# Gated-unit products: weights stationary, or tokens stationary with three products and transposes

## The reference, cut to what matters

```
def swiglu(x, w_gu, w_down):
    g, u = jnp.split(x @ w_gu, 2, axis=-1)      # w_gu: 1024 x 5632
    return (jax.nn.silu(g) * u) @ w_down        # w_down: 2816 x 1024

x = layer_norm(ALPHA * x + 0.5 * swiglu(x, ...), ...)   # four times
```

## Time and profile before

| | us |
|---|---|
| median of 3 runs | 1352.56 (1352.48 to 1353.29) |
| the profiled execution's own time | 1351.47 |
| its span, first to last instruction | 1349.7 |
| PE busy | 1325.7 (98%) |
| PEld busy | 1114.7 (83%) |
| DVE busy | 879.0 (65%) |
| ACT busy | 699.9 (52%) |
| mean granted TensorE clock | 0.997 |

### The profile page before, as it was taken

The page is one execution under the profiler, slowest core; times in us unless marked ns, Lnnn a source line. Parts: engine busy times, 40 slices in busy tenths (PEclk is TensorE's granted clock), DMA queues, the critical chain, the costliest instruction groups (busy, mean ns, idle before and its releaser), DMA issues.

```text
span 1349.7 us, 17387 instructions
## 1 busy us (share of the span) xinstructions
PE 1325.7 (98%) x6757; PEld 1114.7 (83%) x6757; DVE 879.0 (65%) x1214; ACT 699.9 (52%) x1116; POOL 76.1 (6%) x114
## 2 busy tenths in 40 slices
PE   6999999999999999999999999999999999999997
PEld 6788878888888888888877888888888888888885
DVE  6787668777667665665447664676654676766464
ACT  3675564453444554555665553555554544455452
POOL 1401101000002000001001000001000010100000
PEclk9999999999999999999999999999999999999999
DMA  9957754557556655646516556556655565665641
GB/s 349 317 198 242 278 182 162 187 212 257 187 202 192 198 187 185 197 173 225 187 63 218 188 187 211 193 169 219 205 177 183 187 224 182 212 194 187 199 170 69
DMA packets 160222, 268.45 MB, mean 199 GB/s; under 512 B 9755, under 2 KB 103052, under 8 KB 160012
## 3 DMA queue, kind: packets, MB, share of 16 engines
q1 hardware_dynamic: 152428, 239.47, 52.4%
q0 software_dynamic: 7648, 27.85, 5.9%
q10 hardware_dynamic: 64, 0.02, 0.0%
HBM read 266.21 MB, written 1.07 MB: 198 GB/s over the span
## 4 chain that ended last, share of the span: by engine, by line
PE 94%; DVE 2%; DMA 1%; ACT 1%; POOL 1%; issue 0%; SPq 0%; DVEq 0%; ACTq 0%; POOLq 0%
PE TBB L842 12%; PE UPP L842 12%; PE Y L790 10%; PE Y L791 10%; PE Y L792 10%; PE UPP L790 7%; PE UPP L792 7%; PE UPP L791 7%; PE UPP L843 6%; PE TBB L843 6%; PE TBB L887 2%; PE Y L919 1%; DMA WADA<-in_w_ada 1%; PE Y L926 1%; DVE ADA L1847 0%; DMA ADA<-in_b_ada 0%
## 5 line engine op out<-in xcount | busy, mean ns | idle before, releaser
L1726 DVE TENSOR_TENSOR WL<-RAW,WH 128x1024 fp32r<-128x1024 f32 (+2 forms) x438 | 502.3, 1193 | 169.9 <-ACT WH L1307 166.0
L1307 ACT CAST WH<-RAW 128x1024 fp32r<-128x1024 f32 (+2 forms) x438 | 424.6, 1025 | 204.7 <-PE Y L792 73.5
L842 PE MATMUL UPP<-AHL,WH 128*128 128x512 f32 x672 | 240.5, 400 | 0.0
L842 PE MATMUL TBB<-AHL,WH 128*128 128x512 f32 x672 | 239.1, 398 | 0.0
L790 PE MATMUL Y<-WH,HH 128*128 128x512 f32 (+1 forms) x496 | 192.1, 387 | 0.0
L792 PE MATMUL Y<-WH,HL 128*128 128x512 f32 (+1 forms) x496 | 191.4, 386 | 0.0
L791 PE MATMUL Y<-WL,HH 128*128 128x512 f32 (+1 forms) x496 | 191.3, 386 | 0.0
L843 PE MATMUL UPP<-AHL,WL 128*128 128x256 f32 x672 | 188.6, 281 | 0.0
L843 PE MATMUL TBB<-AHL,WL 128*128 128x256 f32 x672 | 188.6, 281 | 0.0
L790 PE MATMUL UPP<-WH,AHL 128*128 128x512 f32 (+1 forms) x448 | 183.1, 409 | 2.4 <-DVE AHL L1880 1.2
L792 PE MATMUL UPP<-WH,AHL 128*128 128x512 f32 (+1 forms) x448 | 174.8, 390 | 0.0
(11 more groups left out here) (258 smaller groups left out, 1370.8 us busy)
## 6 DMA issues: line engine op xcount, KB each, us to landing
RAW<-in_ffn_w_gu SPq DMA_DIRECT2D x176, 512.0 KB, 4.9
RAW<-in_ffn_w_down SPq DMA_DIRECT2D x80, 512.0 KB, 4.3
RAW<-in_w_mlp SPq DMA_DIRECT2D x64, 512.0 KB, 4.4
RAW<-in_w_in SPq DMA_DIRECT2D x34, 512.0 KB, 5.1
PIECE<-in_w_ada POOLq DMA_DIRECT2D x32, 512.0 KB, 5.6
RAW<-in_a_w_in SPq DMA_DIRECT2D x24, 512.0 KB, 4.7
WADA<-in_w_ada SPq DMA_DIRECT2D x14, 512.0 KB, 10.1
RAW<-in_w_out SPq DMA_DIRECT2D x8, 512.0 KB, 4.5
```

The source lines that it names most:

```text
L842: pe.matmul(banks[:, block, :], WH[:, u % 2, w], AHL[:, k, :], start=k == 0, stop=False)
L1307: act.copy(WH[:, u % 2, q * n:(q + 1) * n], raw_half(u, q // 2)[:, (q % 2) * n:(q % 2 + 1) * n]).then_inc(wh_done, 1)
L1726: ve.tensor_tensor(WL[:, u % 2, o], raw_half(u, q // 2)[:, (q % 2) * n:(q % 2 + 1) * n], WH[:, u % 2, o].bitcast(F32), ALU.subtract).then_ ...
```

## The change

One condition. Units named `gu` no longer count as computed by feature; `up` units still do.

```
 def by_feature(key):
 
-    return key[0] in ("up", "gu") and key[:-1] not in PAIRS and (key[0],) + key[1:-2] + (key[-2] - 1,) not in PAIRS
+    return key[0] == "up" and key[:-1] not in PAIRS and (key[0],) + key[1:-2] + (key[-2] - 1,) not in PAIRS
```

## The result

The changed kernel takes 1373.14 us (median of 4 runs, 1370.73 to 1374.27) against 1352.52 (4 runs, 1351.18 to 1353.29). The ratio is 1.0158, interval 1.0146 to 1.0170. Forecast was 1371.0, range 1363 to 1377. The profiled execution took 1373.63 us, its span is 1371.9, 22.2 more than before.

The account below looks back on a forecast made before the run. TensorE, busy for 98% of the span, was taken to set the time through its matmul pace. Pace 2.4, holes at dn 5 12.0 and clock 4.5 summed to 18.9 us, for a median of about 1371.0, range 1363 to 1377.

Parts of the forecast that it names:

- The new wait at dn 5: At dn 5, conversion queues behind the late transposes of gu 10; a 3.00 us hole per layer, 12.0 us in four.
- t + 3.14: Forecast start of dn 5, with t the start of the two late transposes; unhindered it would be t + 0.14.
- dn 0 stays free: At dn 0 the same order costs nothing, because tok 1 of dn 0 follows with 5.44 us more cover.
- Rival (d): A second hole per layer at dn 1 or dn 2 from late transfers, 1 to 3 us a layer, about 1379; chance 0.07.
- The clock: Behind the dn 5 holes the granted clock falls, 1.5 us each, 4.5 us in all; bounds 0 and 6.8.
- my three in four: Forecast share of the four dn 5 holes followed by a clock fall: three, at 1.5 us each.
- The rule of the Trainium skill cited for this: Every wait between bursts brings the clock down; all four holes would pay, 6.0 us in place of 4.5.
- The pace: In gu units 2 to 10, token blocks of 5.69 us replace parts of 5.653: +2.4 us in four layers, bounds 1.0 to 3.9.
- the Trainium skill's per-matmul rule: N / 2.4 GHz plus about 2.5 ns per matmul; estimates +0.09 us a gu block, +6.5 us over 72.
- The sum: Whole kernel: 2.4 + 12.0 + 4.5 = 18.9 us, giving 1370.4 profiled and a median of about 1371.0.
- (b): No hole at dn 5, as ScalarE gets the last rounding done early; only 2.4 us remain, 1355.0; chance 0.05.
- (c): Faster: less ScalarE and VectorE work gives gu blocks of 5.58, saving 5.3 us; 1347 if dn 5 is ready; chance 0.03.

Follow-up runs that it names:

- twelve matmuls: Changed kernel with gu 10's late transposes moved into the middle of dn 4 tok 0, after 12 of its 24 matmuls: 1357.17 us, ratio 1.0049.
- the experiment on one unit: Kernel before with only gu 10 of each layer by tokens, 4 of 36 units: 1368.32 us, ratio 1.0126.
- The constants in the hole: Changed kernel with 15 extra products of constants on TensorE behind the late transposes at dn 4: 1367.49 us, ratio 1.0125.
- The kernel that converts first: Changed kernel with ScalarE and VectorE converting dn 5 before finishing gu 10's late hidden values: 1355.9 us, ratio to before 1.0042.

## Why the prediction was right

The account by layers, changed kernel less kernel before, in us between the same instructions of the two profiles:

| gated layer | 1 | 2 | 3 | 4 | sum |
|---|---|---|---|---|---|
| head of gu 2 to dn 4 | 0.74 | 0.39 | 0.74 | 0.74 | 2.6 |
| dn 4 tok 0, with its transposes | 0.22 | 0.20 | 0.22 | 0.22 | 0.9 |
| hole before dn 5 | 3.00 | 2.99 | 2.99 | 3.00 | 12.0 |
| dn 5 to the end of the layer: the clock, mostly | 1.69 | 1.71 | 1.72 | 1.44 | 6.6 |

**The new wait at dn 5: right in place, mechanism and size.** From the start of the transposes to dn 5 it took 3.14, 3.13, 3.13 and 3.14 us in the four layers; the forecast was t + 3.14, a hole of 3.00 each. It could be that exact because every link was a row of the trace before: the transposes, the copy, the rounding, the subtraction and the release were all there elsewhere, in the same order. One order edit removes it, twelve matmuls shorten it by about their length, and one unit of 36 brings it back.

**That dn 0 stays free: right.** No other wait of TensorE is new. Rival (d) did not come.

**The clock: the mechanism right, the count low in this execution.** All four holes of the profiled execution had a fall of the clock. Behind the first, from 596.00 to the next transposes at 611.98, are 63 matmuls in 15.98 us; the same ones took 14.29 before. The fourth fall began inside its hole, so less of it fell on work, 1.44 us. Together that is 6.6 us where I had put 4.5, just under my upper bound of 6.8. About 0.1 us of each is not the clock but the break: where the experiment on one unit has the hole without a fall, the same 63 matmuls take 14.41 us (595.31 to 609.72). Over executions my three in four is nearer, since the same hole of 3.00 us was followed by a fall or not in one and the same trace: with the experiment on one unit it is six falls at eight holes. Two traces are few for such a share. The constants in the hole show that TensorE's own idleness brings the fall. The rule of the Trainium skill cited for this (TensorE: Matmul & The Clock Gate, section "HAM oscillation — how this bites in real kernels") has every wait of the kernel that it describes bring a fall: this profile agrees, four of four, the experiment with one unit does not, two of four. The Trainium skill gives the waits of its kernel there as about 3 to 5 us, so holes of 3.0 us are at their short end.

**The pace: the mechanism right, the size too low.** The forecast was 0.6 us a layer, 2.4 in all, with an upper bound of 3.9. Measured are 0.96 in layers 1, 3 and 4 and 0.59 in layer 2, 3.5 in all. The term that was mis-sized is the token block, put at 5.69 us. Layer 2 kept to it, with 5.693; the other three had 5.713. The eight blocks of the trace before, 5.68 to 5.71 at the opening of a layer, could not show that a long row of blocks settles at one or the other, and what decides it no run here shows.

The kernel that converts first lies 5.6 us above before (3.9 to 7.4 by its interval), more than this pace. In its own trace the stretches from gu 2 to dn 5 have the same 3.5 us. Its span is 6.5 us longer than that of the kernel before, and 1.9 of these lie ahead of the head of gu 2 in the first layer (448.06 against 446.17), where the granted clock is 0.66 from 20 to 30 us against 0.83. So in that execution over a quarter of the excess is the opening of the program and not the change. How much of the 5.6 us between the medians is so, is not settled. By the Trainium skill's per-matmul rule (TensorE: Matmul & The Clock Gate, section "Wait — 56ns, not 53.3ns?"), as estimated in the prediction, the pace would cost 6.5 us; the traces give 3.5.

**The sum.** 3.5 + 12.0 + 6.6 = 22.1 us against 22.2 between the two spans; 0.2 more lie in the opening of the program, before gu 2 (446.36 against 446.17), and the rest is rounding. By medians it is 20.6 against a forecast of 18.4. There the prediction has a small slip: 1370.4 for the profiled execution and 1.1 for the median make 1371.5, where it says 1371.0. Profile against profile the sum was 3.3 us low (18.9 against 22.2), median against median 2.1. No errors cancel in it: two terms were low, each within its bounds, and the large one was exact. That the medians come nearer than the profiles is chance. Rivals (b) and (c) are out by the four holes; (c) also by the blocks, which with 50 us less work on each of two engines were at 5.693 and 5.713, never under 5.65.

## What to carry to other kernels

When a product's form changes, follow what the other engines' programs wait for, in their written order: a step that used to depend on a neighbour's arithmetic may now depend on the engine whose next input it stands in front of. Ask of every moved dependence what is queued behind it, and give an independent conversion its place ahead of it. A hole of about 3 us in the matmul stream cost its length here and, at six holes of eight, some 1.4 to 1.7 us more at half the clock behind it, so it should be priced with both.

## What the runs showed of the hardware that was not expected

A dense stream of matmuls can run at either of two steady paces with the same instructions. A pair of one 512-column and one 256-column matmul, each with its own weight load, takes 0.3467 us or 0.3533 to 0.3534, and keeps the pace it has for over a hundred pairs, until the stream is interrupted. It is not the granted clock, which is 1.00 in both. One short product of the right width in the stream picks the faster pace for what follows it: 32 columns for one stretch of a gated layer, 72 for the other, with none of the rest of the program changed, 5.9 us in all, the two stretches of the MLP included. Why these widths, and by what state inside TensorE, no run here shows.

The token blocks show the same in small: 5.693 us a block in one gated layer of the changed kernel, 5.713 in the other three. It is not tied to one layer: with gu 10 alone by feature it is the third layer that has 5.69, and the second has 5.71.
